# A two-layer encoder trunk in fp32 halves: the input projection from eight chunks of 268 columns to five column groups of two chunks each

## What is computed

```python
for l in range(DEPTH):                       # DEPTH = 2
    h = rms_norm(x, norm1_g[l])
    (aq, ak, av, bq, bk, bv, cq, ck, cv,
     c_q, c_kv, k_rope) = jnp.split(h @ w_in[l], cuts, axis=-1)
    aq = rms_norm(aq.reshape(B, S, A_HEADS, HEAD_DIM), a_q_norm_g[l])
    ak = rms_norm(ak.reshape(B, S, A_KV_HEADS, HEAD_DIM), a_k_norm_g[l])
    ...                                      # rotary, four attentions o_a, o_b, o_c, o_d
    y = jnp.einsum('bsnc,ncd->bsnd', br, w_branch[l])
    g = jax.nn.sigmoid(h @ w_gate[l] + b_gate[l]).reshape(B, S, N_BRANCH, D)
    x = x + jnp.sum(g * y, axis=2) @ w_o[l]
    h2 = rms_norm(x, norm2_g[l])
    x = x + jnp.square(jax.nn.relu(h2 @ w_ff1[l])) @ w_ff2[l]
return rms_norm(x, final_g)
```

## Time and profile before

| | us |
|---|---|
| time, median of 3 runs (822.63 to 823.55) | 823.1 |
| the profiled execution's own time | 823.43 |
| its span, first to last instruction | 821.6 |
| outside the span | 1.8 |
| granted TensorE clock, mean over the span | 0.998 |

### The profile page before, as it was taken

The page is one execution under the profiler, slowest core; times in us unless marked ns, Lnnn a source line. Parts: engine busy times, 40 slices in busy tenths (PEclk is TensorE's granted clock), DMA queues, the critical chain, the costliest instruction groups (busy, mean ns, idle before and its releaser), DMA issues.

```text
span 821.6 us, 12232 instructions
## 1 busy us (share of the span) xinstructions
PE 809.4 (99%) x4451; PEld 680.6 (83%) x4451; DVE 565.8 (69%) x827; ACT 427.6 (52%) x722; POOL 55.9 (7%) x97
## 2 busy tenths in 40 slices
PE   7999999999999999999999999999999999999996
PEld 7997767877898888888899877677778988888885
DVE  6667767867676766666767677688775676666773
ACT  6455765664354444433564476558544554433442
POOL 2430000000010000000013100000000100000000
PEclk9999999999999999999999999999999999999999
DMA  8976653554357555666556757345344575666541
GB/s 278 228 235 203 182 180 105 143 175 161 110 158 231 171 181 181 202 204 203 173 154 194 243 170 209 101 152 162 109 158 147 182 226 183 204 204 192 179 140 51
DMA packets 85658, 145.12 MB, mean 177 GB/s; under 512 B 5036, under 2 KB 54448, under 8 KB 85616
## 3 DMA queue, kind: packets, MB, share of 16 engines
q1 hardware_dynamic: 82912, 137.12, 52.0%
q0 software_dynamic: 2496, 7.36, 3.4%
q10 hardware_dynamic: 208, 0.08, 0.0%
HBM read 143.49 MB, written 1.05 MB: 176 GB/s over the span
## 4 chain that ended last, share of the span: by engine, by line
PE 94%; DVE 3%; ACT 1%; POOL 1%; DMA 0%; issue 0%; POOLq 0%; ACTq 0%
PE bank_w L1300 14%; PE bank_w L1302 13%; PE bank_w L1301 13%; PE bank_acc L1300 8%; PE bank_acc L1301 8%; PE bank_acc L1302 8%; PE bank_w L1595 5%; PE bank_ox L1595 5%; PE bank_w L1597 3%; PE bank_ox L1597 3%; PE bank_acc L1396 2%; PE bank_ox L1426 2%; PE bank_acc L1409 2%; DVE w_lo L876 2%; DMA cst<-in_table 0%; PE bank_ox L1302 0%
## 5 line engine op out<-in xcount | busy, mean ns | idle before, releaser
L876 DVE TENSOR_TENSOR w_lo<-raw,w_hi 128x1024 fp32r<-128x1024 f32 (+1 forms) x256 | 307.6, 1243 | 56.2 <-ACT w_hi L614 55.8
L614 ACT ACTIVATE w_hi<-raw 128x1024 fp32r<-128x1024 f32 (+1 forms) x256 | 259.5, 1061 | 35.7 <-DMA raw<-in_w_gate 11.9
L1300 PE MATMUL bank_w<-w_hi,act_both 128*128 128x268 f32 (+1 forms) x512 | 178.1, 348 | 0.7 <-DVE act_both L903 0.6
L1302 PE MATMUL bank_w<-w_hi,act_both 128*128 128x268 f32 (+1 forms) x512 | 173.9, 340 | 0.0
L1301 PE MATMUL bank_w<-w_lo,act_both 128*128 128x268 f32 (+1 forms) x512 | 173.7, 339 | 0.0
L1300 PEld LDWEIGHTS bank_w<-w_hi,act_both 128*128 128x128 f32 x512 | 96.2, 188 | 16.8 <-issue 6.0
L1302 PEld LDWEIGHTS bank_w<-w_hi,act_both 128*128 128x128 f32 x512 | 96.2, 188 | 11.1
L1301 PEld LDWEIGHTS bank_w<-w_lo,act_both 128*128 128x128 f32 x512 | 96.3, 188 | 10.2 <-issue 0.5
L1300 PE MATMUL bank_acc<-w_hi,part_hi 128*128 128x512 f32 x256 | 100.2, 391 | 0.0
L1301 PE MATMUL bank_acc<-w_lo,part_hi 128*128 128x512 f32 x256 | 100.1, 391 | 0.0
L1302 PE MATMUL bank_acc<-w_hi,part_lo 128*128 128x512 f32 x256 | 99.9, 390 | 0.0
(11 more groups left out here) (197 smaller groups left out, 1173.8 us busy)
## 6 DMA issues: line engine op xcount, KB each, us to landing
raw<-in_w_ff SPq DMA_DIRECT2D x128, 512.0 KB, 4.6
raw<-in_w_gate SPq DMA_DIRECT2D x64, 512.0 KB, 4.7
raw<-in_w_in SPq DMA_DIRECT2D x32, 536.0 KB, 5.5
raw<-in_w_o SPq DMA_DIRECT2D x16, 512.0 KB, 4.6
gate_row<-in_b_gate POOLq DMA_DIRECT2D x16, 256.0 KB, 4.4
raw<-in_w_branch SPq DMA_DIRECT2D x16, 256.0 KB, 4.5
raw<-in_w_branch SPq DMA_DIRECT2D x8, 512.0 KB, 4.5
xs<-in_x SPq DMA_DIRECT2D x2, 512.0 KB, 4.2
```

Source lines behind the costliest of these rows:

```text
L614: nc.scalar.activation(half_view(w_hi, c, h), raw_half(c, h), ACT.Copy).then_inc(w_hi_ready, 1)
L876: nc.vector.tensor_tensor(half_view(w_lo, c, hf), raw_half(c, hf), f32(half_view(w_hi, c, hf)), ALU.subtract).then_inc(w_lo_ready, 1)
L1300: nc.tensor.matmul(dst, s_hi, m_hi, start=first, stop=False)
L1302: ins = nc.tensor.matmul(dst, s_lo, m_hi, start=False, stop=last)
```

## The change

The columns are cut at the branches into five groups g: 512, 384, 384, 512 and 352 columns wide (B is cut in two). A group has two chunks, 2g with the row slices 0 to 3 and 2g+1 with the slices 4 to 7, so there are ten `in` chunks and ten steps. Step s computes one token tile of one group: tile s % 2 of group s // 2, with both chunks of the group. On tile 0 TensorE waits for the first chunk ahead of the first twelve matmuls and for the second chunk ahead of the other twelve. Both chunks are given back during tile 1. ACT copies tile 0's result in even steps, DVE tile 1's in odd ones. The steps of all later work move back by two; `a_squares`, `a_norm` and `a_rotate` stay at s = 2, 3 and 4, and POOL's waits stay at hi(3) to hi(7). A layer now has 66 chunks, no multiple of the ring of four, so the place in the ring is counted over the layers (`slot`).

```diff
-IN_N = 8
-IN_C = IN_W // IN_N
+IN_AT = [AQ, BQ, (BQ + CQ) // 2, CQ, DCQ, IN_W]
+IN_G = len(IN_AT) - 1
+IN_N = 2 * IN_G
...
-SCORES, SOFTMAX, TURN, VALUES, HEAD_OUT = 8, 9, 10, 11, 12
+SCORES, SOFTMAX, TURN, VALUES, HEAD_OUT = 10, 11, 12, 13, 14
...
-SPLIT_AT[0:IN_N + 1] = [[]] + [[s + 2] for s in range(1, IN_N - 1)] + [[IN_N + 1, IN_N + 2], [IN_N + AHEAD]]
+SPLIT_AT[0:IN_N + 1] = [[3], []] + [[s + 2] for s in range(2, IN_N - 1)] + [[IN_N + 1, IN_N + 2], [IN_N + AHEAD]]
...
 # SyncE
+                elif kind == "in":
+                    k = KD // 2 * (i % 2) + 2 * h
+                    src = w_in.rearrange("l (k p) n -> l p k n", p=P)[l, :, k:k + 2, IN_AT[i // 2]:IN_AT[i // 2 + 1]]
+                    sp.dma_start(dst.rearrange("p (k n) -> p k n", k=2), src).then_inc(done, 16)
...
 # ScalarE, step s
-                    if kind == "in" and j:
-                        in_evac(j, l)
+                    if kind == "in" and j and j % 2 == 0:
+                        in_evac(j // 2, l)
...
 # VectorE, step s
-                    if kind == "in":
+                    if kind == "in" and j % 2:
                         dve.wait_ge(w_used, used_count(l, j))
-                        nc.vector.tensor_copy(qkv[:, 1, j * IN_C:(j + 1) * IN_C],
-                                              bank_w[:, in_bank(j, 1, l), 0:IN_C]).then_inc(in_dve, 1)
+                        nc.vector.tensor_copy(qkv[:, 1, IN_AT[j // 2]:IN_AT[j // 2 + 1]],
+                                              in_bank(j // 2, 1, l)).then_inc(in_dve, 1)
                     if s == 0 and l == 0:
                         split_lo(2, 0)
                     if s == 3:
                         a_norm(l)
...
 # TensorE
-            def project_both(j, l):
-
-                pe.wait_ge(w_lo_ready, lo_count(l, j))
-                pe.wait_ge(in_act, l * IN_N + j)
-                if j == 2:
-                    pe.wait_ge(in_dve, l * IN_N + 1)
-                project(j, 0, l)
-                pe.wait_ge(in_dve, l * IN_N + j)
-                project(j, 1, l)
+            def project_part(g, t, l, half, ks=range(KD // 2), lo_counts=None):
+
+                c, tok = 2 * g + half, slice(t * P, (t + 1) * P)
+                hi, lo = k_view(w_hi, c, KD // 2, l), k_view(w_lo, c, KD // 2, l)
+                kcs = [half * KD // 2 + k for k in ks]
+                sides = [(act_hi[:, kc, tok], act_lo[:, kc, tok], hi[:, k, :], lo[:, k, :]) for k, kc in zip(ks, kcs)]
+                ins = split_product(in_bank(g, t, l), sides, kcs[0] == 0, kcs[-1] == KD - 1, lo_counts)
+                if t == T - 1 and ks[-1] == KD // 2 - 1:
+                    ins.then_inc(w_used, 1)
+                elif kcs[-1] == KD - 1:
+                    ins.then_inc(in_half, 1)
+            def project(g, t, l):
+
+                if l or g > 1:
+                    pe.wait_ge((in_act, in_dve)[t], l * IN_G + g)
+                for half in range(2):
+                    if t == 0:
+                        pe.wait_ge(w_lo_ready, lo_count(l, 2 * g + half))
+                    project_part(g, t, l, half)
...
-                        project_both(j, l)
+                        project(j // 2, j % 2, l)
```

More of the change, by code:

```diff
@@ L68 @@
 AHEAD = 3
-WMAX = KD * IN_C
-assert NC % RING == 0 and NC % RAW == 0
+WMAX = 2048
+assert NC % RAW == 0
 MLP_LOOP = POS["f1", 1]
@@ L378, in chunk_cols, with in_width, in_bank, slot @@
         def chunk_cols(c):
[L379 to L386, removed]
+            kind, j = CHUNKS[c]
+            return KD // 2 * in_width(j // 2) if kind == "in" else 2048
+        def in_width(g):
+            return IN_AT[g + 1] - IN_AT[g]
+        def in_bank(g, t, l):
+            return (bank_w[:, t, :] if l or g else bank_acc[:, 2 + t, :])[:, 0:in_width(g)]
+        def slot(c, l):
+            return (l * NC + c) % RING
+        def split_view(buf, c, l):
+            return buf[:, slot(c, l), 0:chunk_cols(c)]
         def gate_slot(n, q):
@@ L767, in _ @@
             act.wait_ge(vec_ready, 1)
[L768 to L772, removed]
+            turned_hi_both(0, G1, 0, (0, 1))
+            for kc in range(2, KD, 2):
+                split_hi_half(kc // 4, kc // 2 % 2, 0)
+                turned_hi_both(0, G1, 0, (kc, kc + 1))
             split_hi(2, 0)
@@ L1159, in _ @@
             dve.wait_ge(vec_ready, 1)
[L1160 to L1164, removed]
+            for kc in range(0, KD, 2):
+                split_lo_half(kc // 4, kc // 2 % 2, 0)
+                turned_lo_both(0, G1, 0, (kc, kc + 1))
             for l in range(DEPTH):
@@ L1429, in values @@
                             ins.then_inc(pv_done, 1)
[L1431 to L1438, removed]
@@ L1454, in project_next_layer @@
+            def project_first_layer():
+                for kc in range(0, KD, 2):
+                    half, k = divmod(kc, KD // 2)
+                    pe.wait_ge(w_lo_ready, kc // 2 + 1 + 2 * RAW)
+                    project_part(0, 0, 0, half, (k, k + 1), [2 * (kc + 1), 2 * (kc + 2)])
+                    project_part(0, 1, 0, half, (k, k + 1))
             def project_next_layer(l):
-                left, right = range(0, KD // 2), range(KD // 2, KD)
                 base = 2 * l * 2 * KD
+                counts = [base + kc + 1 for kc in range(2 * KD)]
@@ L1489, in bank_free, with feature_block @@
                     pe.wait_ge(y_read, l * 16 + (4 * n + q + 1))
-            def feature_block(dst, c, d, kcs=range(KD), lo_counts=None):
-                hi, lo = k_view(w_hi, c, KD), k_view(w_lo, c, KD)
+            def feature_block(dst, c, d, l, kcs=range(KD), lo_counts=None):
+                hi, lo = k_view(w_hi, c, KD, l), k_view(w_lo, c, KD, l)
                 sides = [(hi[:, kc, d * P:(d + 1) * P], lo[:, kc, d * P:(d + 1) * P], act_hi[:, kc, :], act_lo[:, kc, :])
@@ L1551, in last_branch, with token_sum @@
                 turn_mix(1, l)
-            def token_sum(c, a_hi, a_lo, p, start, stop, ks=(0, 1)):
-                hi, lo = k_view(w_hi, c, 2), k_view(w_lo, c, 2)
+            def token_sum(c, l, a_hi, a_lo, p, start, stop, ks=(0, 1)):
+                hi, lo = k_view(w_hi, c, 2, l), k_view(w_lo, c, 2, l)
                 t, a, b = p
```

106 lines of the change are left out of this document (46 added, 60 removed), and 6 rows, old and new, of the table X_AT.

## The result

The changed kernel takes 841.68 us (median of six runs, 838.96 to 844.45) against 823.33 (six runs, 822.63 to 823.71): a ratio of 1.0224, 95% interval 1.0194 to 1.0255. It is slower by 2.2%; the forecast was 836.9, 1.7%, with a range of 828.0 to 843.5. The profiled execution took 843.71, 20.3 more than the profiled one of before.

A forecast was written before the change was run, and what follows sets the result against it. PE was taken to bound the kernel throughout. Terms -1.6 - 0.2 + 0.6 + 9.7 + 5.3 = +13.8 us on the profiled 823.4 gave 837.2, or 836.9 against the median, slower by 1.7%; range 828 to 843.5.

The forecast's parts named there:

- the place and the chain: Projection: lo(5) late behind POOL's root, copy and a_norm, lo(7) behind POOL's additions; PE waits in middle of steps 4, 6.
- faster: Rival: both lo are there when PE comes mid-steps 4 and 6, only products count; -1.8, 821.3 us; chance 0.07.
- light stalls: Rival: rs_a is in time and POOL's additions miss lo(7); sum +5.6, 828.7 us; chance 0.17.
- The products, -1.6: Projection on PE: fewer, wider products save cost per instruction, 0.8 us a layer; -1.6, bounds 0 and -2.4.
- The start, -0.2: Both layers' starts: halves of the first chunks shrink from 1072 to 1024 columns, so DVE is waited for less; -0.2 us.
- Chunk 9, +0.6: PE waits for DVE's lo(9), 2.6 against transposes of 0.35 and 1.93; 0.3 per layer, +0.6 us (0 to 1.2).
- Chunk 11: First gate: DVE's 3.1 us against transposes of 0.35 and 2.8; no stall before, none now.
- Chunk 5, +9.7: Step 4: lo(5) late behind POOL's root, copy and a_norm; stall 4.8 us per layer, +9.7 (3.0 to 6.2 bounds).
- I take 3.5: POOL's root for rs_a, ahead of a_norm and lo(5): taken as 3.5 us, between about 2.9 alone and 4.7 before.
- Chunk 7, +5.3: Step 6: lo(7) late, meeting POOL's four bias additions; 1.3 + 4.0, +5.3 us (0.8 to 8.0).
- one layer of each kind, as the trace has them: Step 6: in one layer half of lo(7) stands behind one addition, in the other behind all four; 1.3 + 4.0 us.
- The clock: Rival: PE standing nearly 5 us in step 4 drops the clock; 839.5 us for one layer, 842.1 both; chance 0.2.

The follow-up runs named there:

- Experiments 4 to 6: Experiment 4: changed kernel, with POOL's four bias additions waiting until lo(7) is done; 834.07 us, ratio 1.0126. Experiments 5 and 6 have their own lines.
- Experiment 8: Lo made a step earlier on DVE, a_rotate and additions later, with weight ring and load buffer places 2144 columns wide instead of 2048; 824.13 us, ratio 1.0013.
- experiment 1: The changed kernel run again with no edit, to see how far its times repeat; 841.82 us, ratio 1.0216.
- experiment 5: Changed kernel, with POOL taking A's root before its wait for hi(4) and the first bias DMA; 836.24 us (831.26 to 841.16), ratio 1.0174.
- experiment 3: Changed kernel, with 16 throwaway products (32 matmuls, 3.5 us) on PE ahead of the second-chunk waits in steps 4 and 6; 836.75 us, ratio 1.0166.
- experiments 2, 3 and 5: Experiment 2: changed kernel, with 33 throwaway products (7.3 us) ahead of the second-chunk waits in steps 4 and 6; 850.13 us. Experiments 3 and 5 have their own lines.
- experiment 6: Changed kernel, with POOL's additions waiting for lo(7) and DVE making lo(5) ahead of a_norm in step 3; 825.25 us, ratio 1.0026.

## Why the prediction was right, and where not

**Right: the place and the chain.** "PE wants that chunk in the middle of step s+1": all four stops are there, and none at the gates. Experiments 4 to 6 took the named causes away one at a time, and the stops went with them. The *faster* rival fell at its own place, the two waits in the middle of steps 4 and 6; *light stalls* fell as both its conditions, rs_a in time and additions that miss lo(7), failed in the trace.

**The products, -1.6: measured -2.4.** The 384s came out at 0.173 (forecast 0.175), the 352s at 0.159 (0.161), but the 512s at 0.227, not the 0.231 of the earlier trace rows. Experiment 8 shows that this last part belongs to the ring's place size, a part of the change that the forecast did not price. For 288 products it is 8 ns each; the fixed cost of about 2.5 ns that the Trainium skill's "TensorE: Matmul & The Clock Gate" gives ("Wait — 56ns, not 53.3ns?") would make an estimated 0.7, so the rows bear out the choice against it. The start, -0.2, measured -0.7, but it moves from execution to execution: 10.91 here, 11.64 in experiment 1, 11.59 before.

**Chunk 9, +0.6: measured 0.4.** Chunk 11: none, as forecast. Two bounds do not follow from their own figures: 47.46 - 46.41 = 1.05 per layer makes -2.1 and not -2.4 (so the measured -2.4 lies outside that bound), and with the root of 4.7 that the rows give, the upper bound of chunk 5 is 6.0 and not 6.2. Neither is in the sum.

**Chunk 5, +9.7: measured 8.4** (4.2 in each layer). The step that was off is the root: "I take 3.5", while it took 2.9 (29.18 to 32.09), as the bound without DVE's copy had it. With it in time, experiment 5 gives 3.0: copy 0.47, a_norm 2.53 and lo(5) 1.88 against 0.47, 2.52 and 1.95.

**Chunk 7, +5.3: measured 7.4.** The step that failed is "one layer of each kind, as the trace has them": both layers were of the bad kind, which the forecast had as its upper bound of 8.0. The clock did that (experiment 3): in all six layers traced with step 5 at the full clock and the additions in place (experiments 2, 3 and 5) the meeting is of the good kind, and where no throwaways fill it the stop is 1.0 (experiment 5). So without the fall chunk 7 would have come to some 2.0, an estimate from that trace.

**The clock, left out of the sum: measured +8.7** in the profiled execution, and some 5 more that it put on chunk 7 (7.4 against 2.0). It was a rival with a chance of 0.2, and its condition, "if PE stands for nearly 5 us in step 4", was set too high: it fell in stops of 4.2 and, in experiment 5, of 3.0, also in step 6, so that it fell four times, not twice; each fall of the changed kernel cost 1.7 to 2.7, the latter close to the 2.6 that the rival took. In waits of 1.7 (experiment 6) and 1.0 (experiment 5) it did not fall. This agrees with the Trainium skill, the same page, "HAM oscillation — how this bites in real kernels": waits between bursts let the next one start at half rate. The argument against it, "a slower PE also gives DVE and POOL time ahead of chunk 7", went the wrong way: the slower step 5 released lo(7) later, into the additions. This was the term to put into the sum: with stalls of 4.8 us forecast, the trace of before already had an idle PE at clock 0.53.

Against the forecast 837.2, then: clock +8.7, chunk 7 +2.1, chunk 5 -1.3, products -0.8, start -0.5, transposes -0.3, chunk 9 -0.2, and the rest of layer 0 -1.2: +6.5, as in 843.7 - 837.2. That the median stayed inside the range is in part luck. By the forecast's own prices the case that came, a fallen clock in both layers (842.1) and both meetings bad (+2.7), is 844.8 and lies above it; misses of +10.8 and -4.3 cancelled in part.

## What to carry to other kernels

Where a change splits a step, move every queue's release with it: here products got cheaper by 2.4 us, and operands that were due half a step earlier cost 24, stops and clock together. A forecast stop of the size seen here, 3.0 to 4.2 us, belongs in the sum twice, as itself and as the slower products behind it; and a slowed step also moves what other queues release from its end, here lo(7) into POOL's additions. When a wait goes, look at once for the next in line: lo(5), then lo(6), then a load behind a table were each late in turn.

## What the runs showed of the hardware

- Four additions on POOL and a subtraction on DVE hold each other up: a half of lo(7) stands behind one addition (3.10 in place of 2.35 for both halves) or all four (5.79). Twelve meetings were traced. In seven a half had begun 0.5 to 0.8 us ahead of the first addition, and lo(7) took 3.1 to 3.2; in five a half began between 0.3 us ahead of it and 0.2 behind it, and lo(7) took 5.7 to 6.2. Why is open.
- The granted clock went from 2.4 to 1.2 GHz at each of the twelve traced stops of 3.0 to 4.2 us inside the kernel, and at none of the shorter waits of the projection, 1.7 us at most; constant products in the stop kept it up at no change to the work.
- The size of a place in the weight ring and load buffer (2048 or 2144 columns) moves the distance of 512-column products by 2.4 ns and, the other way, that of a 512 and 256 pair by 2. The cause was not looked for.
- An fp32 product of 128 columns shows as two matmuls of 0.11 us; it is not one like the fp32r ones.
- A load of a weight half took 9.1 us to land with a bias table's DMA beside it; with that table and w_uq moved behind it 7.6, and ACT waited 0.2, not 2.0.
